# Expert layers of a two-block transformer: a ring of 18 weight halves in place of 16, scatter tables and gates built pair by pair

## What is computed

```
def hier_moe(x, w_grp, b_grp, w_exp, b_exp, w_gate, w_up, w_down):
    ...
        g_sel = jnp.argmax(pg, -1)
        ...
        top_p, top_i = lax.top_k(pe, TOPK_IN_GROUP)
        ...
        gate = jnp.sum(jax.nn.one_hot(eid, N_EXPERTS, dtype=jnp.float32)
                       * (g_prob[:, None] * top_p)[..., None], axis=1)
        hdn = jax.nn.silu(jnp.einsum('sd,edf->sef', xs, w_gate)) * jnp.einsum('sd,edf->sef', xs, w_up)
        hdn = hdn * gate[..., None].astype(hdn.dtype)
        return jnp.einsum('sef,efd->sd', hdn, w_down)
```

## Time and profile before

| | |
|---|---|
| median of 3 runs | 1136.83 us (1132.68 to 1138.58) |
| profiled execution: its own time | 1128.46 us |
| profiled execution: span, first to last instruction | 1126.3 us |
| mean granted TensorE clock, of full speed | 0.989 |
| busy: PE / DVE / ACT / POOL | 92% / 42% / 33% / 10% |
| experts of layer 0: first gather to last down product | 538.0 to 757.2 us |
| experts of layer 1 | 891.0 to 1110.1 us |

### The profile page before, as it was taken

The page is one execution under the profiler, slowest core; times in us unless marked ns, Lnnn a source line. Parts: engine busy times, 40 slices in busy tenths (PEclk is TensorE's granted clock), DMA queues, the critical chain, the costliest instruction groups (busy, mean ns, idle before and its releaser), DMA issues.

```text
span 1126.3 us, 15330 instructions
## 1 busy us (share of the span) xinstructions
PE 1038.6 (92%) x6021; PEld 709.2 (63%) x6021; DVE 468.0 (42%) x973; ACT 374.5 (33%) x725; POOL 111.5 (10%) x147
## 2 busy tenths in 40 slices
PE   6999999999998999899999999888889999999884
PEld 6967799999867888567543434337557644344332
DVE  4644656665456445757310101016765611111004
ACT  4454455555344354852110101013472211111100
POOL 0621011111001000430000000000141000000000
PEclk9999999999999999999999999999999999999998
DMA  9843675554455416029699999992417499999993
GB/s 335 214 151 113 206 233 188 168 206 153 147 184 189 140 72 243 2 102 423 276 411 421 420 421 422 419 397 86 175 79 299 189 408 422 421 420 421 420 415 132
DMA packets 93920, 296.94 MB, mean 264 GB/s; under 512 B 9950, under 2 KB 42894, under 8 KB 70286
## 3 DMA queue, kind: packets, MB, share of 16 engines
q1 hardware_dynamic: 92254, 290.08, 67.2%
q0 software_dynamic: 1584, 5.77, 1.3%
HBM read 294.58 MB, written 1.25 MB: 263 GB/s over the span
## 4 chain that ended last, share of the span: by engine, by line
PE 71%; DMA 13%; DVE 8%; ACT 4%; issue 3%; SPq 0%; POOL 0%; POOLq 0%; ACTq 0%; DVEq 0%
PE ps L839 33%; PE ps L1201 14%; PE ps L1232 7%; DMA w<-in_moe_w_up 5%; DMA hT<-in_moe_w_down 3%; DMA w<-in_moe_w_down 3%; DMA arena<-in_moe_w_down 2%; PE ps L1185 2%; PE ps L941 2%; PE ps L910 2%; PE ps L920 1%; PE ps L1245 1%; PE ps L833 1%; PE ps L780 1%; PE ps L787 1%
## 5 line engine op out<-in xcount | busy, mean ns | idle before, releaser
L1440 DVE TENSOR_TENSOR plo<-w,phi 128x1024 fp32r<-128x1024 f32 (+3 forms) x143 | 174.5, 1235 | 160.7 <-ACT phi L2067 159.5
L2067 ACT CAST phi<-w 128x1024 fp32r<-128x1024 f32 (+3 forms) x143 | 144.6, 1028 | 169.3 <-PE ps L839 155.7
L1201 PE MATMUL ps<-w,arena 128*64 128x512 f32 x656 | 171.1, 595 | 8.7 <-DMA w<-in_moe_w_up 5.7
L839 PE MATMUL ps<-hTr,phi 128*128 128x256 f32 x472 | 134.1, 284 | 1.8 <-DVE yTr L1430 1.8
L839 PE MATMUL ps<-hTr,plo 128*128 128x256 f32 x472 | 133.7, 283 | 0.0
L839 PE MATMUL ps<-yTr,phi 128*128 128x256 f32 x472 | 133.7, 283 | 0.0
L1925 DVE SCALAR_TENSOR_TENSOR yTr<-ps,small,yTr 128x512 fp32r<-128x512 f32 x32 | 22.7, 747 | 240.9 <-ACT yTr L2306 240.9
L1201 PEld LDWEIGHTS ps<-w,arena 128*64 128x64 f32 x656 | 53.9, 137 | 97.4 <-issue 96.4
L839 PE MATMUL ps<-phi,hTr 128*128 128x512 f32 (+2 forms) x240 | 94.3, 393 | 4.5 <-DVE yTr L1430 4.5
L839 PE MATMUL ps<-phi,yTr 128*128 128x512 f32 (+2 forms) x240 | 93.6, 390 | 3.5 <-issue 1.9
L839 PEld LDWEIGHTS ps<-hTr,phi 128*128 128x128 f32 x472 | 90.7, 192 | 2.1 <-DVE yTr L1430 2.0
(11 more groups left out here) (299 smaller groups left out, 1606.1 us busy)
## 6 DMA issues: line engine op xcount, KB each, us to landing
w<-in_moe_w_gate SPq DMA_DIRECT2D x42, 1024.0 KB, 16.0
w<-in_moe_w_up SPq DMA_DIRECT2D x40, 1024.0 KB, 19.5
w<-in_moe_w_down SPq DMA_DIRECT2D x38, 1024.0 KB, 19.4
w<-in_w_up SPq DMA_DIRECT2D x22, 1024.0 KB, 7.5
arena<-in_moe_w_up SPq DMA_DIRECT2D x20, 1024.0 KB, 17.1
arena<-in_moe_w_gate SPq DMA_DIRECT2D x20, 1024.0 KB, 19.6
arena<-in_moe_w_down SPq DMA_DIRECT2D x20, 1024.0 KB, 19.4
w<-in_w_out SPq DMA_DIRECT2D x6, 2048.0 KB, 8.6
```

The lines of the kernel that those rows point to most:

```text
L839: ins_ = e.matmul(o, l[a], r[b], start=first and i == 0, stop=last and i == 2, skip_group_check=group)
L1201: ins_ = e.matmul(bank[64 * ee:64 * ee + 64, :], xg[:, k, o:o + 64], half_view(kind, p, ee, ab)[:, c, :], start=(k == 0), stop=(k == 7))
L1440: e.tensor_tensor(plo[:, 0:m], slots[u % 3][:, j * m:j * m + m], phi[:, 0:m].bitcast(F32), ALU.subtract).then_inc(s_cut)
L2067: e.copy(pieces[p % 4][0][:, 0:m], slots[u % 3][:, j * m:j * m + m]).then_inc(s_cast)
```

## The change

`NHALF` becomes 18. The two more places are `ring[:, 1024:3072]` (place 9) and `ring[:, 3072:5120]` (place 17); `ring` grows by 1024 columns, `small` shrinks by 136 (the tile `sgt` moves into `ang`), and the hidden layer and its transposed tile have one buffer each, `middle` and `turned`. The tables and gates are made for one pair at a time: `slots_of(p)` on TensorE, behind `down(p - 1)` (for p = 0 behind `project("u", 0)`), with the result in bank 0 of PSUM, and `keep_slots(p)` on VectorE, which copies them to a table of two buffers, `hots` (in the memory of `mv` of layer 0), and to a column of `slot_gate`. `slots_of` reads the four-expert table `one_hots` that the gather already has, so `all_places` goes. New waits: the next pair's `project("g")` waits for `keep_slots` of this pair (they share bank 0), and every `keep_down` and `scatter` for its own pair's. Half 9 is issued with the arena's, half 17 when the router's products that read `xT` are done. The branch `many_tokens`, which does not run here, gets other buffers.

```
-NHALF = 16
+NHALF = 18
...
+        halves += [ring[:, 1024:3072]]
         halves += [slots[i][:, h * 2048:h * 2048 + 2048] for i in (2, 3, 4) for h in range(2)]
-        halves += [hT[:, :, :].rearrange("p c t -> p (c t)")]
-        xT = ring[:, 2048:4096].rearrange("p (c t) -> p c t", c=KC)
-        bts = [hots_r[:, p * 256:p * 256 + 256] for p in range(8)]
-        Hb = [Lb[0], Pb[2]]
+        halves += [hT[:, :, :].rearrange("p c t -> p (c t)"), ring[:, 3072:5120]]
+        xT = ring[:, 3072:5120].rearrange("p (c t) -> p c t", c=KC)
+        logits = ring[0:20, 512:768]
+        turned, middle = ring[:, 0:512], ring[:, 512:1024]
...
                     elif n == 4:
                         e.wait_ge(s_pv, (48, 80)[i])
-                    elif n == 9:
+                    elif n == 10:
                         e.wait_ge(*consumed(held[2]))
-                    elif n == 11:
+                    elif n == 12:
                         e.wait_ge(s_pc, 2 * units[name_of[held[2]]]["pieces"][1])
+                    elif n == 17:
+                        e.wait_ge(*B.full(f"lg{i}1", 0))
                     expert_half(i, n)
...
                     if after:
-                        e.wait_ge(s["wf"], last_use(9, 10))
+                        e.wait_ge(s["wf"], last_use(10, 11))
                         load(after[2], False)
...
                 def project(kind, p, bank):
 
+                    if kind == "g" and p:
+                        e.wait_ge(s["bb"], p)
+                        e.wait_ge(s["gv"], 2 * p)
...
-                        if kind == "u" and p == 0:
-                            slot_gates(4 * ab, 4 * ab + 4)
...
+                def slots_of(p):
+
+                    e.wait_ge(s["sl"], p + 1)
                     e.wait_ge(s_gate, i + 1)
+                    table = [one_hots[:, t, p % 2 * 128:p % 2 * 128 + 128].bitcast(F32) for t in range(2)]
+                    for t in range(2):
+                        e.transpose(psum[0][:, t * 128:t * 128 + 128], table[t], ident)
+                    for t in range(2):
+                        ins_ = e.matmul(psum[0][:, 256:258], table[t], gate[:, t, 2 * p:2 * p + 2],
+                                        start=(t == 0), stop=(t == 1))
+                    ins_.then_inc(s["wb"])
...
                     if p:
                         down(p - 1)
+                        slots_of(p)
                         e.wait_ge(s["ht"], p)
                     project("u", p, psum[1])
                     if p == 0:
+                        slots_of(p)
...
+                def keep_slots(p):
+                    e.wait_ge(s["wb"], p + 1)
+                    if p >= 2:
+                        e.wait_ge(s["sc"], 2 * (p - 2) + 2)
+                    e.tensor_copy(hots[:, p % 2, :], psum[0][:, 0:256]).then_inc(s["bb"])
+                    for ee in range(2):
+                        e.tensor_copy(slot_gate[64 * ee:64 * ee + 64, p:p + 1],
+                                      psum[0][64 * ee:64 * ee + 64, 256 + ee:257 + ee]).then_inc(s["gv"])
...
                     e.wait_ge(s["wf"], block_done("g", p))
-                    if p >= 2:
-                        e.wait_ge(s["tf"], p - 1)
-                    e.activation(Hb[p % 2], psum[0][:, :], ACT.Silu).then_inc(s["sl"])
+                    if p:
+                        e.wait_ge(s["tf"], p)
+                    e.activation(middle, psum[0][:, :], ACT.Silu).then_inc(s["sl"])
...
                     e.wait_ge(s["tf"], p + 1)
-                    if p >= 2:
-                        e.wait_ge(s["wf"], block_done("d", p - 2))
-                    e.copy(Pb[p % 2][:, :], psum[1][:, :]).then_inc(s["ht"])
+                    if p:
+                        e.wait_ge(s["wf"], block_done("d", p - 1))
+                    e.copy(turned, psum[1][:, :]).then_inc(s["ht"])
```

More of the change, by code:

```diff
@@ L231, in build @@
         arena = sb("arena", [128, 12360])
[L232 to L235, removed]
+        ring = sb("ring", [128, 5120])
         Pb, Tb = ([ring[:, b + i * 512:b + i * 512 + 512] for i in range(3)] for b in (0, 2048))
         Lb = [ring[:, b:b + 512] for b in (1536, 3584)]
-        small = sb("small", [128, 1600])
+        small = sb("small", [128, 1464])
         with ExitStack() as same:
@@ L241, in build @@
         mkT = sb("mkT", [128, 2, 2, T])
+        with ExitStack() as same:
+            hots = same.enter_context(nc.sbuf_tensor("hots", [128, 2, T], F32R))
         mv = sb("mv", [128, 2, 2, T])
@@ L307, in build @@
         halves += [arena[:, 2048 + i * 2048:4096 + i * 2048] for i in range(5)]
+        halves += [ring[:, 1024:3072]]
         halves += [slots[i][:, h * 2048:h * 2048 + 2048] for i in (2, 3, 4) for h in range(2)]
-        halves += [hT[:, :, :].rearrange("p c t -> p (c t)")]
-        xT = ring[:, 2048:4096].rearrange("p (c t) -> p c t", c=KC)
-        bts = [hots_r[:, p * 256:p * 256 + 256] for p in range(8)]
-        Hb = [Lb[0], Pb[2]]
[L313 to L317, removed]
+        halves += [hT[:, :, :].rearrange("p c t -> p (c t)"), ring[:, 3072:5120]]
+        xT = ring[:, 3072:5120].rearrange("p (c t) -> p c t", c=KC)
+        logits = ring[0:20, 512:768]
+        turned, middle = ring[:, 0:512], ring[:, 512:1024]
+        xT_all = z[:, :, :].rearrange("p t d -> p (t d)").rearrange("p (c t) -> p c t", c=KC)
+        gbcs = [gain_rows[:, i * 256:i * 256 + 256] for i in range(2)]
+        gT = gain_rows[:, 512:768]
+        tms = [gain_rows[:, 768 + i * 256:1024 + i * 256] for i in range(3)]
         ar_at[0] = 0
@@ L356, in build @@
         tmp4 = [sm(96) for _ in range(4)]
[L357 removed]
+        sgt = ang.rearrange("p k n -> p (k n)").rearrange("p (t n) -> p t n", t=2)
         hs = sm(2)
@@ L1930, in few_tokens @@
                 keep(0, 1)
-                all_places()
                 for p in range(8):
                     if p:
+                        keep_slots(p)
                         if p in (1, 3, 5):
@@ L1939, in few_tokens @@
                     e.wait_ge(s["wf"], block_done("u", p))
-                    e.tensor_tensor(Hb[p % 2], Hb[p % 2], psum[1][:, :], ALU.mult).then_inc(s["hm"])
+                    e.tensor_tensor(middle, middle, psum[1][:, :], ALU.mult).then_inc(s["hm"])
                     if p == 0:
-                        e.wait_ge(s["gg"], 2)
-                        for ee in range(2):
-                            e.tensor_copy(slot_gate[64 * ee:64 * ee + 64, :],
-                                          psum[7][64 * ee:64 * ee + 64, ee:16:2]).then_inc(s["gv"])
-                        for b in (2, 3):
-                            e.wait_ge(s["wb"], b + 1)
-                            e.tensor_copy(hots_r[:, b * 512:b * 512 + 512], psum[4 + b][:, :]).then_inc(s["bb"])
+                        keep_slots(0)
                     if p in (1, 3, 5):
@@ L2312, in few_tokens @@
                     e.wait_ge(s["wf"], block_done("g", p))
-                    if p >= 2:
-                        e.wait_ge(s["tf"], p - 1)
-                    e.activation(Hb[p % 2], psum[0][:, :], ACT.Silu).then_inc(s["sl"])
+                    if p:
+                        e.wait_ge(s["tf"], p)
+                    e.activation(middle, psum[0][:, :], ACT.Silu).then_inc(s["sl"])
                     if p:
                         keep_down(p - 1)
-                    else:
-                        for b in range(2):
-                            e.wait_ge(s["wb"], b + 1)
-                            e.copy(hots_r[:, b * 512:b * 512 + 512], psum[4 + b][:, :]).then_inc(s["ba"])
                     if p in (1, 3, 5):
```

50 lines of the change are left out of this document (11 added, 39 removed).

## The result

| | before | after |
|---|---|---|
| median of the compared executions | 1135.74 us (1132.68 to 1138.58, 4) | 1117.76 us (1116.74 to 1118.70, 4) |
| ratio, with its 95% interval | | 0.9842 (0.9813 to 0.9871) |
| profiled execution: own time, span, mean clock | 1128.46, 1126.3, 0.989 | 1118.70, 1116.9, 0.986 |
| first gather to last down product, layer 0 / layer 1 | 219.2 / 219.1 us | 212.5 / 213.0 us |

In two later comparisons the same kernel came to ratios of 0.9885 and 0.991, with 0.9903 forecast; the median of all 15 executions of after is 1120.2 us. So there are two questions: what the mechanism gave, and why comparisons of the same two kernels differ by several us.

The account below looks back on a forecast made before the run. The weight stream was taken to bound the expert layers. 5.0 us for two halves plus 0.5 for the dip made 5.5 a layer, 11.0 in both: 1136.8 to 1125.8 us, range 1119 to 1133.

Parts of the forecast that it names:

- The stream sets the end: Expert layers: each ends when weight half 95 lands, at about 419 GB/s, plus an unchanged 3.67 us of down product.
- Two more halves ahead: Pause before each layer's experts: two more halves load there, 2.50 us each, so the stream ends 5.0 us earlier.
- The dip: Stream at 567 to 568 and 921 to 922 us: the briefly empty queue no longer occurs, 0.5 us a layer.
- The TensorE margin: TensorE's idle time in each layer's last part: 11.6 and 10.7 us before, 6.1 and 5.2 after the change.
- TensorE's small blocks: Gate products and transposes spread over the pairs: 0.70 us each, 5.56 leaving pair 0 and 5.6 returning, sum 0.
- keep_slots: VectorE's copies during project("u", p): at most 2.1 us a pair, covered by idle time, cost 0.
- single buffers: One buffer each for the hidden layer and its transposed tile: both new waits already over when reached, cost 0.
- the next layer's weights: Loads into the ring of 18: still behind half 95 in the same queue, moving with the stream, cost 0.
- The base, 1136.8: Median of the runs before the change, 8.4 us above the profiled execution, from which 11.0 us was subtracted.
- TensorE as the bound: Rival, chance 0.10: small blocks cost more and exceed TensorE's idle time; at 1.0 us more a pair, 1130.5 us.
- only half of the gain arrives, or none: Two rivals: one layer or place gains, 1131.3 us, chance 0.09; stream as long as before, 1136.8, chance 0.04.
- slower: Rival, chance 0.06: keep_slots delays VectorE's queue; at 2.2 us a pair 12.9 us slower, 1149.7 us.

Follow-up runs that it names:

- the repeat: The kernel before, unchanged, run and profiled a second time: 1131.06 us, ratio 1.0001, layer 0's experts 219.2 us.
- The 12 fillers: The changed kernel with 16 halves plus 12 filler products behind slots_of(0): one execution, 1131.16 us, layer 0's experts 218.5 us.
- an empty queue: The changed kernel with 16 halves plus 22 filler products behind slots_of(0): 1138.72 us, ratio 1.0062, layer 0's experts 222.3 us.
- fillers outside it: The changed kernel with layer 0's 16 end fillers moved behind the branch, and 14 instead of 9 in the router's wait: 1122.75 us, ratio 0.9901.
- Without fillers: The changed kernel without the 16 filler products at the end of layer 0's experts: 1116.07 us, ratio 0.9858, four executions.

## Why the prediction was right in kind and short in size

**The stream sets the end: right.** Rate 420, chain through half 95, one microsecond of stream is one microsecond of layer (4.4 lost, 4.7 later).

**Two more halves ahead, 5.0 us a layer: right.** 2.8 + 2.2 = 5.0 measured in layer 0, 2.7 + 2.0 in layer 1. The Trainium skill's 358 GB/s a core (Perfetto Trace Analysis, Roofline), by which the two places would be an estimated 5.9, is its figure for two cores that share the memory. This program runs on one core, and 5.0 is the sum by the trace's 419.

**The dip, 0.5 us a layer: mis-sized.** The work pair by pair gave 1.6 us. I read the dip from the one microsecond at 197 GB/s. It is spread over four or five, and cost 0.8 us in the profiled execution of before and 1.2 in the repeat, by the same reckoning. The 12 fillers, which put project("g", 1) where it stood in before, bring back 0.85 of the 1.6, and lose 0.9 us of stream. The other 0.4 to 0.8 us are open. In layer 1 the work pair by pair gave 1.0 to 1.2 us. The TensorE margin came out lower too, 4.7 and 4.6 for 6.1 and 5.2.

**TensorE's small blocks, 0.70 us a pair: right,** 0.37 + 0.34 us in the chain. **keep_slots, single buffers, the next layer's weights at nothing: right, as far as the profiles show.** The experts took what the stream took, in pair 1 4.26 us of idle time stand behind keep_slots, and m0's cast stands at 757.40 against the layer norm's end at 761.7. The sum has no term for the 0.7 us that the end of the program got longer.

**The step that failed: "The median of the runs lies 8.4 us above the profiled execution; from it the same sum gives" 1125.8.** I carried that offset over as if it belonged to the kernel. It belongs to the clock of the executions: before's profiled one ran at 0.989, which only 2 of its 65 later ones reached. The clocks of the three others are not recorded; at 1132.7 to 1138.6 us they lie where later executions had 0.977 to 0.985. The 8.0 us between 1125.8 and 1117.76 come apart so. The base, 1136.8, lies 4.2 above the median of all later executions of before, 1132.6. The gain is 12.4 and not 11.0 between the medians of all executions, 1132.6 and 1120.2; the experts alone give 6.7 + 6.1 = 12.8. And the four executions of after in the first comparison ran at 0.986 to 0.988, 2.4 us below the median of all 15. 4.2 + 1.4 + 2.4 = 8.0. So 6.6 of the 8.0 us are the draw of three executions of before and four of after, and 1.4 the change. Both draws went the same way; that was chance, and by the median of all 15 executions, 1120.2, after lies 5.6 below the forecast. The sum against the profiled execution, span 1115.3, was 1.6 off (1116.9) at a clock 0.003 lower, with the errors on both sides that stand under the chain of waits above.

Shown by runs: each place's worth, the cost of an empty queue, the margin, the tie between clock and time. Only argued: that the low stretches follow TensorE's idle gaps. Open: why one execution loses the clock at a place and the next does not, whether after draws higher clocks than before (means 0.985 and 0.983), and the 0.7 us at the program's end.

**The rivals.** TensorE as the bound does not occur, but it is 4.7 us of work a layer away, and two more halves, 5.0 us, would already be more than that. That only half of the gain arrives, or none, is excluded by the two places' 2.8 and 2.2 us; slower, by VectorE's idle time and the result.

## What to carry to other kernels

When a stream of weights sets the end and its queue stands still for lack of places, count what stands still: each place filled in that time is worth one transfer, until the waiting engine's own idle time is used up. Read a dip in the rate over all the microseconds in which it is below the plateau, not in the worst one.

Where executions of a kernel spread by 1%, set each against its mean clock before carrying an offset from one kernel to another. A length inside the program that the clock doesn't touch, here first gather to last down product, tells in one execution what medians of five can't.

## What the runs showed of the hardware

- The time follows the mean granted clock at some 0.9 us per 0.001: 1128.6 to 1140.3 us over 65 executions of before at 0.990 to 0.976, 1116.6 to 1126.6 over 15 of after at 0.990 to 0.979. Stretches at the lower level come and go between executions of one kernel, at places that no edit touches.
- On the way out of the branch TensorE did nothing for 3.60 us (after) and 3.94 us (before) behind fillers inside it, and for 6.39 us ahead of fillers outside it, with nothing in the profile that it waited for. Without fillers the transposes started 0.09 us behind the layer norm, so there the way out is hidden by the layer norm.
- One place more in the ring took 2.8 and 2.2 us from an expert layer (a transfer of 1024 KB takes 2.50 at 419 GB/s), and 4.4 us in which the queue was empty made it 4.7 us longer.
- A filler product of 128x256 float32 costs 0.44 us at the full clock, in two records (22 of them 9.6 us), and 0.57 us partly at the lower one (16 in 9.15 us).
